# Moving three steps of a state-space scan by one or two weight units in a single-core Trainium2 kernel

## What is computed

```
xs, bm, cm = split(silu(conv(x @ w_in[:, D_INNER:])))      # 64 heads x 64, and 8 groups x 128 twice
cb     = einsum("bcqgn,bcsgn->bgcqs", c_c, b_c)             # products of C and B, one set per group
y_diag = einsum("bgcqs,bgrcqs,bcsgrp->bcqgrp", cb, decay_in, xs*dt)
y      = y_diag + y_off + xs * d_skip
y      = y * silu(z)                                        # z = x @ w_in[:, :D_INNER]
y      = y * rsqrt(mean(y*y over the 512 columns of a group) + eps) * norm_w
out    = y @ w_out
```

## Time and profile before

| what | us |
|---|---|
| median of 3 runs | 2149.06 (2148.76 to 2149.56) |
| the profiled execution's own time | 2148.38 |
| its span, first to last instruction | 2146.7 |
| PE busy in the span | 2135.5 (99%) |
| DVE / ACT / POOL busy | 1360.7 / 1082.5 / 131.4 |
| one group of the scan (group 4, from the first matmul of its unit 0 on) | 28.73 |

### The profile page before, as it was taken

The page is one execution under the profiler, slowest core; times in us unless marked ns, Lnnn a source line. Parts: engine busy times, 40 slices in busy tenths (PEclk is TensorE's granted clock), DMA queues, the critical chain, the costliest instruction groups (busy, mean ns, idle before and its releaser), DMA issues.

```text
span 2146.7 us, 32636 instructions
## 1 busy us (share of the span) xinstructions
PE 2135.5 (99%) x12180; PEld 1853.2 (86%) x12180; DVE 1360.7 (63%) x1677; ACT 1082.5 (50%) x1422; POOL 131.4 (6%) x152
## 2 busy tenths in 40 slices
PE   9999999999999999999999999999999999999999
PEld 9988899999888878988888888888888888888887
DVE  6677777777545767765777665555645555555554
ACT  4544467786433455663444555454434434443442
POOL 2000001111000100000024300000000000000000
PEclk9999999999999999999999999999999999999999
DMA  7577766655665754457576554556666666656654
GB/s 249 180 204 211 211 206 187 186 175 169 228 194 181 228 165 148 153 182 212 181 215 186 167 157 138 167 172 193 191 192 192 187 195 190 188 192 194 189 189 164
DMA packets 206533, 403.05 MB, mean 188 GB/s; under 512 B 15408, under 2 KB 17904, under 8 KB 206144
## 3 DMA queue, kind: packets, MB, share of 16 engines
q1 hardware_dynamic: 198976, 385.53, 57.3%
q0 software_dynamic: 4512, 14.57, 3.1%
q10 hardware_dynamic: 2912, 1.06, 0.2%
HBM read 395.27 MB, written 5.83 MB: 187 GB/s over the span
## 4 chain that ended last, share of the span: by engine, by line
PE 95%; DVE 3%; ACT 1%; issue 0%; DMA 0%; POOL 0%; DVEq 0%; ACTq 0%
PE ps L417 16%; PE ps L419 16%; PE ps L418 16%; PE ps L396 14%; PE ps L401 7%; PE ps L383 6%; PE ps L384 6%; PE ps L385 6%; DVE xbc L1647 1%; PE ps L1212 1%; DVE wlo L370 1%; PE ps L1396 1%; PE ps L1419 1%; PE ps L1512 1%; PE ps L1486 1%; ACT whi L365 0%
## 5 line engine op out<-in xcount | busy, mean ns | idle before, releaser
L370 DVE TENSOR_TENSOR wlo<-raw,whi 128x1024 fp32r<-128x1024 f32 x712 | 873.7, 1233 | 700.5 <-ACT whi L365 696.7
L365 ACT ACTIVATE whi<-raw 128x1024 fp32r<-128x1024 f32 x712 | 753.8, 1060 | 996.8 <-PE ps L419 562.9
L396 PE MATMUL ps<-xhl,whi 128*128 128x512 f32 x1472 | 369.3, 393 | 0.9 <-DVE wlo L370 0.4
L383 PE MATMUL ps<-xhl,whi 128*128 128x256 f32 x1088 | 313.9, 289 | 0.9 <-DVE wlo L370 0.9
L396 PEld LDWEIGHTS ps<-xhl,whi 128*128 128x128 f32 x1472 | 264.8, 189 | 50.1 <-DVE wlo L370 1.9
L384 PE MATMUL ps<-xhl,whi 128*128 128x256 f32 x1088 | 307.6, 283 | 0.0
L385 PE MATMUL ps<-xhl,wlo 128*128 128x256 f32 x1088 | 307.6, 283 | 0.0
L417 PE MATMUL ps<-whi,xhl 128*128 128x512 f32 x756 | 301.9, 399 | 0.5 <-DVE xhl L1909 0.5
L419 PE MATMUL ps<-whi,xhl 128*128 128x512 f32 x756 | 294.8, 390 | 0.0
L418 PE MATMUL ps<-wlo,xhl 128*128 128x512 f32 x756 | 294.6, 390 | 0.0
L401 PEld LDWEIGHTS ps<-xhl,wlo 128*128 128x128 f32 x1472 | 200.8, 190 | 14.4
(11 more groups left out here) (273 smaller groups left out, 2086.9 us busy)
## 6 DMA issues: line engine op xcount, KB each, us to landing
raw<-w SPq DMA_DIRECT2D x256, 512.0 KB, 4.3
raw<-w_in SPq DMA_DIRECT2D x160, 512.0 KB, 4.5
raw<-w_qkv SPq DMA_DIRECT2D x96, 512.0 KB, 3.7
raw<-w_out SPq DMA_DIRECT2D x64, 512.0 KB, 4.7
raw<-b_in SPq DMA_DIRECT2D x64, 512.0 KB, 3.7
raw<-b_out SPq DMA_DIRECT2D x32, 512.0 KB, 4.5
raw<-w_o SPq DMA_DIRECT2D x32, 512.0 KB, 3.7
cumb<-cum_scratch SPq DMA_DIRECT2D x16, 512.0 KB, 4.2
```

Of the source, the lines that this page charges most:

```text
L365: act.activation(whi[:, u % RING], raw[:, u % RING], ACT.Copy).then_inc(S("hi_ready"), 1)
L370: dve.tensor_tensor(wlo[:, u % RING], raw[:, u % RING], whi[:, u % RING].bitcast(F32), ALU.subtract).then_inc(S("lo_ready"), 1)
L383: pe.matmul(o, w_h, ah[:, k, :], start=(k == 0 and n % 2 == 0), stop=False, skip_group_check=True)
L396: pe.matmul(ps[:, bank + n, :], whi[:, u % RING, t, n * P:(n + 1) * P], both, start=(k == 0), stop=False, skip_group_check=True)
```

## The change

PE: `states` goes from behind unit 2 to behind unit 3 and there behind the two `y_pair`; the second `inputs_turned` goes from behind unit 6 to behind unit 7, and there behind `y_pair` and `spread_rstd`. DVE: `states_masked` goes from slot 3 to slot 4, where `y_read` twice stands ahead of it; the second `inputs_scaled` goes from slot 7 to slot 0 of the next group, behind its `y_read`. Everything else keeps its place, and no instruction is added or removed.

```diff
@@ group(g), PE
                     if j in y_at:
                         for e in range(2):
                             y_pair(PAIRS * g + 2 * y_at.index(j) + e)
+                    if g > 0 and j == SPREAD_AT:
+                        spread_rstd(g - 1)
                     if g + 1 < GROUPS:
-                        if j == 2:
+                        if j == 3:
                             states(g + 1)
                         if j == 4:
                             inputs_turned(g + 1, 0)
-                        if j == 6:
+                        if j == 7:
                             inputs_turned(g + 1, 1)
-                    if g > 0:
-                        if j == SUM_AT:
-                            square_sum(g - 1)
-                        if j == SPREAD_AT:
-                            spread_rstd(g - 1)
+                    if g > 0 and j == SUM_AT:
+                        square_sum(g - 1)
@@ the scan's slots, DVE
+                    if g > 0 and j == 0:
+                        inputs_scaled(g, 1)
                     if g + 1 < GROUPS:
-                        if j in (5, 7):
-                            inputs_scaled(g + 1, j // 2 - 2)
-                        if j == 3:
+                        if j == 5:
+                            inputs_scaled(g + 1, 0)
+                        if j == 4:
                             states_masked(g + 1)
                     split_lo(dve, Z + g * UPP + RING + j, 0)
```

## The result

The changed kernel takes 2156.48 us (median of 7 runs, 2156.08 to 2156.78) against 2149.07 us (median of 7, 2148.76 to 2149.56): the ratio is 1.0034, 95% interval 1.0024 to 1.0044, or 7.4 us more. The prediction said 2156.4. The profiled execution took 2156.30 with a span of 2154.6, 7.9 us above that of before.

A forecast was written before the change was run, and what follows sets the result against it. PE, busy 99% of the span, was taken to bound the kernel. Waits of 6.45 + 0.93 = 7.38 us, less 0 for seams, on the 2149.06 median gave 2156.4 us, range 2153.6 to 2158.9.

The forecast's parts named there:

- PE bound, nothing absorbs a wait: In the scan PE is busy 28.73 of 28.73 us, so any wait put on it is lost time.
- Seams at 0: New neighbours among PE's small pieces save nothing; upper bound 14 x 0.1 = 1.4 us, taken as 0.
- the 7.38: Summed waits at the sum of squares: 5 x 1.29 in groups 2 to 6 plus 0.93 in group 1, in us.
- The y blocks: Both blocks stand earlier on PE, by 0.65 and 0.44 us, without waiting; margins about 0.3 and 0.15 us.
- The scaling in slot 0: DVE's second input scaling, 0.69 us, fits in its 1.40 us wait for ACT ahead of the split; cost 0.
- The mask: Behind slot 3's split and two reads of y, it delays PE's sum of squares 1.29 us, in group 1 0.93.
- The split beside POOL: DVE's slot 3 split takes 1.50 us to the next start beside POOL in groups 2 to 6; undisturbed 1.14.
- the first: Mask ready by about 420.33, no wait at the sum of squares: 2147.7 to 2149.1 us, chance 0.08.
- The second: Faster by over 0.2%, though PE's seams could gain 1.4 us at most, giving 2147.7 us; chance 0.02.
- The third: PE's y blocks wait too, about 0.2 us in each of 12: 2.4 us more, 2158.8 us, chance 0.06.
- The fourth: DVE's split does no work until POOL is done: 8.1 us in all, 2157.2 us, chance 0.05.
- a wait neither grows nor heals: PE's wait stays the same size from group to group, since ACT's and DVE's slots hang on PE's units.

The follow-up runs named there:

- the forced delay: Against the changed kernel with the mask back in slot 3: first input scaling of groups 1 to 6 moved behind slot 6's split; 2151.50 us against 2148.89, ratio 1.0012.
- the first experiment: Changed kernel with DVE making the mask in slot 3 again, PE keeping the new order; 2148.34 us against 2148.79, ratio 0.9998.
- the fourth experiment: Kernel before with only the second turn behind unit 7 and the second scaling in slot 0; 2148.70 us against 2148.79, ratio 0.9999.

## Why the prediction was right, point by point

- **PE bound, nothing absorbs a wait.** Right. The waits reached the end in full: 7.6 us in the pieces of the changed kernel and 7.6 between the medians where the mask alone was moved. Of the 7.9 between the two spans some 0.4 lie behind PE's last matmul, which starts 7.5 later (2150.18 against 2142.65).
- **Seams at 0.** Right: 2.30 and 2.53 are the sums of their parts. In group 0 the seam of y and turn saved some 0.05 us.
- **A term that is missing.** The prediction took 0.65 for the products of C and B at every place. In group 0 they cost 0.98 before, with a wait that the view of the matmuls' waits doesn't list and the weight loads' view does, and the change gives these 0.33 us back. The waits came out 0.26 above the 7.38 (7.64). The two nearly cancel, so that 2156.4 met 2156.48 to 0.1 us is in part luck; the mechanism and its size don't hang on it.
- **The y blocks.** Right that they don't wait, and right that the room was small; the forced delay put it at 0.1 us, where I had said about 0.15.
- **The scaling in slot 0.** Right, shown by the first and the fourth experiment.
- **The mask.** The step that carries the sum held in its place, its count and its size. ACT's end of rounding sets the split, and group 7 before was a true copy of the new list: 1.57, 0.86, 0.55 came back. The load starts 1.31 us late where I said 1.29, in group 1 0.97 instead of 0.93. The mis-sized term is the release. I took 0.04 from POOL's sum to the load; from DVE's mask it is 0.11 (424.99 to 425.10). The trace of before had that number, at the wait of group 0 shown above (297.33 to 297.44).
- **The split beside POOL.** Its measured 1.57 against 1.23 is what put groups 2 to 6 above group 1 (1.31 against 0.97). The stretch follows the overlap with POOL: here the split starts 0.48 ahead of POOL's end (422.65) and steps 1.49, 0.35 more than the undisturbed 1.14; with the mask in slot 3 it starts 0.22 ahead (in group 3 of the first experiment, 390.05) and steps 1.22, 0.08 more. Both are the overlap less 0.14 or so. The Trainium skill (SBUF — State Buffer, "SBUF: two separate sides") has the later of the two blocked in full until the earlier ends. A full block would have stepped the split to 422.65 + 1.14 = 423.79, 0.13 later than the 423.66 of the row, so the trace agrees with a lock but for this constant.
- **Rivals.** The mask came too late by far for the first. The second failed for the reason given. The third didn't come: no wait stands at L1212. The fourth, POOL's lock in full, had the right mechanism and was 0.13 us a group too high.
- **A premise that held here only by size.** I said that a wait neither grows nor heals. True of waits of 1.3 us. With 2.8 us it cost about half as much again through the clock, and my rule for pricing a wait (its length) would have been 8.9 us short.

## What to carry to other kernels

A bound engine's idle time can hide in an order written by hand: moving an instruction one slot later also moves it behind whatever else stands in that slot, here a split that couldn't start before ACT's 418.74 and two reads. Look for a stretch of the same trace that already runs the new list (here the last group, which has no mask) and shift its rows by the period; that gave 1.29 for a measured 1.31. And ask why two steps are tied before moving one: the reader waited for a PSUM bank, not for data, and two columns elsewhere made the late mask free.

## What the runs showed of the hardware

- The granted clock answers to short waits. With six waits of 0.97 to 1.3 us it stayed at full; with waits of 1.55 to 1.9 us it was at half for part of one group of six (share 0.57 over 4.0 us) in the profiled execution; with waits of 2.8 us it was at half behind four of six, and this cost 8.9 us on top of 16.8 us of waiting. I hadn't expected this of a PE whose matmuls have no other wait in these groups.
- Putting small fp32 pieces side by side between units of fp32r matmuls saves nothing: four transposes cost 0.44 alone and beside others, and two pieces side by side cost the sum of both within 0.02, but for 0.05 at y and turn in group 0.
- A VectorE subtraction of two SBUF tiles that starts while GpSimd's add still runs gets longer by the overlap less some 0.14 us (0.22 gave 0.08, 0.48 gave 0.35). One that starts ahead of GpSimd's (L370 at 418.62, POOL's L606 at 419.00) keeps its 1.22.
- From the end of a DVE instruction to the weight load that waited for it took 0.11 us at the sum of squares and at the products of C and B, and 0.06 (432.07 to 432.13) in the middle of a y block.
